# First mixers' loop: sigmoids from tanh, and the norms' inverse roots as a power on GpSimd

## What is computed

```
w  = -softplus(-(w0 + tanh(w_lo) @ w_up)) - 0.5 ; decay = exp(-exp(w))   # = exp(DECAY * sigmoid(w0 + ..))
a  = sigmoid(a0 + a_lo @ a_up)
g  = sigmoid(g_lo) @ g_up
kk = k * k_k ; kk = kk / max(sqrt(sum(kk * kk)), 1e-12)          # per head of 64
k  = k * (1 + (a - 1) * k_a) ; b_vec = kk * a
y  = recurrence over positions of (r, k, v, decay, -kk, b_vec)
y  = (head_norm(y) + bonus) * g                                  # head_norm: yc * rsqrt(mean(yc^2) + eps) * gain
ret = silu(gate_in) * head_norm(retention(q, k, v))
```

## Time and profile before

| | us |
|---|---|
| three runs | 2713.27, 2714.29, 2707.25; median 2713.27 |
| the profiled execution's own time | 2706.05 |
| its span | 2704.3 |
| busy over the span: TensorE matmul, VectorE, ScalarE, GpSimd | 2523.2, 1959.6, 1408.6, 595.2 |
| same in 500 to 600 us, two mixer turns and a part of a third | 89.75, 84.75, 80.24, 67.07 |

### The profile page before, as it was taken

One profiled execution on the slowest core, in us unless ns is written; L12 is line 12 of the kernel. 1 busy time (PEld: TensorE's weight loads), 2 busy tenths in 40 slices (PEclk: granted clock), 3 DMA queues, 4 the chain that ended last, 5 costly groups with the idle time before them and its releaser, 6 DMA issues. The chain is left out here.

```text
span 2704.3 us, 39668 instructions
## 1 busy us (share of the span) xinstructions
PE 2523.2 (93%) x14812; PEld 2065.1 (76%) x14813; DVE 1959.6 (72%) x2659; ACT 1408.6 (52%) x2172; POOL 595.2 (22%) x554
## 2 busy tenths in 40 slices
PE   8999978989897899999996899889999999999998
PEld 7988846666676688888885888668887788888776
DVE  5533147888845799999996834778778988888586
ACT  5111157787612687887785432357744433344444
POOL 0000035666601100000001500320001333432231
PEclk9999989999997899999998999999999999999999
DMA  5555321211263799999996321000221232325866
GB/s 187 192 202 219 123 90 36 74 44 63 84 236 137 278 419 412 412 412 418 414 416 228 133 60 45 1 33 32 57 94 55 78 93 62 93 86 173 208 132 183
DMA packets 168279, 454.06 MB, mean 168 GB/s; under 512 B 15260, under 2 KB 95568, under 8 KB 154832
## 3 DMA queue, kind: packets, MB, share of 16 engines
q1 hardware_dynamic: 146048, 384.62, 38.7%
q0 software_dynamic: 16336, 46.67, 6.3%
q10 hardware_dynamic: 5760, 20.97, 1.9%
HBM read 373.05 MB, written 79.17 MB: 167 GB/s over the span
## 5 line engine op out<-in xcount | busy, mean ns | idle before, releaser
L135 PE MATMUL psum<-part,expert_x_high 128*128 128x512 f32 x520 | 206.5, 397 | 2.9 <-issue 1.5
L137 PE MATMUL psum<-part,expert_x_low 128*128 128x512 f32 x520 | 203.5, 391 | 0.0
L135 PE MATMUL psum<-project_w_high,high 128*128 128x448 f32 (+1 forms) x512 | 194.6, 380 | 3.5 <-DVE low L399 3.5
L136 PE MATMUL psum<-project_w_low,high 128*128 128x448 f32 (+1 forms) x512 | 193.7, 378 | 0.0
L137 PE MATMUL psum<-project_w_high,low 128*128 128x448 f32 (+1 forms) x512 | 193.6, 378 | 0.0
L130 DVE TENSOR_TENSOR expert_down_low<-expert_down,expert_down_high 128x2048 fp32r<-128x2048 f32 x62 | 139.3, 2289 | 36.0 <-ACT expert_down_high L125 36.0
L130 DVE TENSOR_TENSOR expert_gate_low<-expert_gate,part 128x2048 fp32r<-128x2048 f32 x64 | 143.9, 2289 | 6.9 <-ACT part L125 6.2
L130 DVE TENSOR_TENSOR expert_up_low<-expert_up,part 128x2048 fp32r<-128x2048 f32 x64 | 143.8, 2289 | 1.0 <-ACT part L125 1.0
L135 PE MATMUL psum<-part,ffn_w_high 128*128 128x512 f32 x352 | 138.5, 394 | 4.1 <-DVE ffn_u L4694 3.8
L136 PE MATMUL psum<-ffn_b_low,ffn_w_high 128*128 128x512 f32 x352 | 137.9, 392 | 0.0
L135 PE MATMUL psum<-down_right_high,down_left_high 128*128 128x512 f32 x308 | 121.8, 395 | 9.5 <-DVE down_right_low L130 6.0
(11 more groups left out here) (772 smaller groups left out, 7457.5 us busy)
## 6 DMA issues: line engine op xcount, KB each, us to landing
expert_gate<-in_w_gate_dram SPq DMA_DIRECT2D x32, 2048.0 KB
expert_up<-in_w_up_dram SPq DMA_DIRECT2D x32, 2048.0 KB, 9.8
expert_down<-in_w_down_dram SPq DMA_DIRECT2D x32, 2048.0 KB, 10.7
ffn_w<-in_ffn_w_up_dram SPq DMA_DIRECT2D x44, 512.0 KB, 4.6
y_rows<-expert_y ACTq DMA_DIRECT2D x32, 512.0 KB, 10.8
down_right_raw<-in_ffn_w_down_dram SPq DMA_DIRECT2D x44, 256.0 KB, 3.7
hidden_rows<-ffn_hidden SPq DMA_DIRECT2D x20, 512.0 KB, 2.8
ffn_hidden<-hidden_rows SPq DMA_DIRECT2D x20, 512.0 KB, 6.9
```

The source lines that it names most:

```text
L135: pe.matmul(out, left[0], right[0], start=start, stop=False)
L136: pe.matmul(out, left[0], right[1], start=False, stop=False)
L137: return pe.matmul(out, left[1], right[0], start=False, stop=stop)
```

## The change

Every sigmoid of the loop becomes `0.5 * (1 + tanh(x/2))`: ScalarE takes Tanh with scale 0.5, and the missing `+1` and `0.5` are put elsewhere. For `g`, `take_lo` is now two copies, the second adding 1, and `take_g` halves. For `a`, `k_a` is halved once, `rated_b` adds the 1 in a fused operation and `tildes_ba` halves. For the decay, the 1 becomes a bias of the exponentials, from a new constant `decay_bias`. For the gate, a second ScalarE pass adds 1 in place, and `ret_gain` is halved once. The three `warm_up` calls of a turn are gone.

The three square roots of a turn leave ScalarE, and the maximum, mean-plus-eps and reciprocal steps leave VectorE. GpSimd does in their place, for each, an add or maximum and a `tensor_tensor` with `ALU.pow` against a tile of -0.5, 8 or 4 columns wide. `root_kk(t+1)` stands on GpSimd between `scale_m` and `weigh`; `rw_deviation(t-1)` and `ret_deviation(t-1)` between `open_gate` and `rw_leave`. VectorE's divide is one fused product with the square root of the width. ScalarE's y_fm copy, which overwrites the squares, and square_ret get explicit waits for the sums. The last tile's norms stay as they were.

```diff
@@ VectorE
             def unit_kk(j, u, link):
-                v.wait_ge(kk_root, 2 * j + u + 1)
-                link(v.tensor_scalar(kk_stats[:, 1, :], kk_stats[:, 1, :], 1e-12, None, ALU.max))
-                link(v.reciprocal(kk_stats[:, 2, :], kk_stats[:, 1, :]))
+                v.wait_ge(kk_root, 2 * (2 * j + u) + 2)
...
-                link(v.tensor_tensor(b_[:], kk[:], ag[:], ALU.mult))
+                link(v.scalar_tensor_tensor(out=b_[:], in0=ag[:], scalar=1.0, in1=kk[:], op0=ALU.add, op1=ALU.mult))
...
-            def spread(link, of, stats, heads, width, eps, spread_ready):
-                link(v.tensor_reduce(stats[:, 2, 0:heads], three(of, heads), AX_X, ALU.add))
-                v.tensor_scalar(stats[:, 3, 0:heads], stats[:, 2, 0:heads], 1.0 / width, eps, ALU.mult, ALU.add)\
-                    .then_inc(spread_ready, 1)
+            def spread(of, stats, heads, spread_ready):
+                v.tensor_reduce(stats[:, 2, 0:heads], three(of, heads), AX_X, ALU.add).then_inc(spread_ready, 1)
+
+            def divide(stats, heads, width, out, normed):
+                v.scalar_tensor_tensor(out=three(out, heads), in0=three(out, heads), scalar=float(np.sqrt(width)),
+                                       in1=per_row(stats[:, 5, 0:heads], width), op0=ALU.mult, op1=ALU.mult).then_inc(normed, 1)
...
             def rw_divide(t, link):
-                v.wait_ge(rw_root, t + 1)
-                norm_divide(v, link, rw_stats, RW_HEADS, RW_N, y[:], rw_normed)
+                v.wait_ge(rw_root, 2 * t + 2)
+                divide(rw_stats, RW_HEADS, RW_N, y[:], rw_normed)
...
             v.wait_ge(const, 16 * len(cn.loads))
+            v.tensor_scalar(k_a[:], k_a[:], 0.5, None, ALU.mult).then_inc(halved, 1)
@@ GpSimd
+            def root(stats, heads, add, op, t, ready):
+                of = stats[:, 2, 0:heads]
+                pool.tensor_scalar(of, of, add, None, op).then_inc(ready, 1)
+                pool.wait_ge(ready, 2 * t + 1)
+                pool.tensor_tensor(stats[:, 5, 0:heads], of, half_down[:, 0:heads], ALU.pow).then_inc(ready, 1)
...
                 scale_m(t, u)
+                if not last:
+                    root_kk(t + 1)
                 weigh(t, u)
...
                 open_gate(t, u)
                 if not first:
+                    rw_deviation(t - 1)
+                    ret_deviation(t - 1)
                     rw_leave(t - 1, 1 - u)
@@ ScalarE
             def take_lo(j, u):
                 act.wait_ge(lo_turned, 2 * j + u + 1)
-                act.activation(lo_t[:], bank[7][:, 0:256], ACT.Copy).then_inc(lo_t_ready, 1)
+                act.activation(lo_t[:, 0:P], bank[7][:, 0:P], ACT.Copy)
+                act.activation(lo_t[:, P:2 * P], bank[7][:, P:2 * P], ACT.Identity, bias=1.0).then_inc(lo_t_ready, 1)
...
-                act.activation(sg[:], p_t[:], ACT.Sigmoid).then_inc(sg_ready, 1)
+                act.activation(sg[:], p_t[:], ACT.Tanh, scale=0.5).then_inc(sg_ready, 1)
...
-                act.activation(p_t[:], bank[6][:], ACT.Exp, scale=DECAY).then_inc(exp_ready, 1)
+                act.activation(p_t[:], bank[6][:], ACT.Exp, scale=DECAY / 2, bias=decay_bias[:, 0:1]).then_inc(exp_ready, 1)
...
-                if not last:
-                    warm_up(ACT.Exp)
-                else:
+                if last:
                     early_high_of(3)
...
                     reach_ends(t + 1, 1 - u)
-                    root_kk(t + 1)
...
-                warm_up(ACT.Sigmoid)
                 act.wait_ge(q_turned, t + 1)
                 act.activation(q1[:], bank[7][:], ACT.Copy).then_inc(q1_ready, 1)
...
-                act.activation(gate[u][:], ret_in[u][:, 3 * RET_W:4 * RET_W], ACT.Sigmoid).then_inc(gate_opened, 1)
+                act.activation(gate[u][:], ret_in[u][:, 3 * RET_W:4 * RET_W], ACT.Tanh, scale=0.5).then_inc(gate_turned, 1)
                 act.wait_ge(u_made, t + 1)
                 act.activation(u_[:], bank[1][:], ACT.Copy).then_inc(u_ready, 1)
+                act.wait_ge(gate_turned, t + 1)
+                act.activation(gate[u][:], gate[u][:], ACT.Identity, bias=1.0).then_inc(gate_opened, 1)
...
-                if not first:
-                    rw_deviation(t - 1)
...
-                if not first:
-                    ret_deviation(t - 1)
                 act.wait_ge(y_made, t + 1)
+                if not first:
+                    act.wait_ge(rw_spread, t)
                 act.activation(y_fm[:], two_banks(2)[:, :, 1, :], ACT.Copy).then_inc(y_fm_ready, 1)
```

More of the change, by code:

```diff
@@ L480, in __init__ @@
         ]
-        sb("start", [P, 40])
+        sb("start", [P, 32])
         self.loaded = nc.alloc_semaphore(name="mix_consts_loaded")
@@ L905, in mean_square, with divide_last @@
                     steps[0] += 1
-                def divide(raw, stats, heads, width, n):
+                def divide_last(raw, stats, heads, width, n):
                     v.wait_ge(last_root, n)
@@ L1034, in _ @@
             sigmoid_arg_a(0, 0)
+            v.wait_ge(halved, 1)
             link = rated(0, 0)
@@ L1075, in square_kk, with root_kk, rw_deviation, ret_deviation @@
                 pool.tensor_tensor(b_[:], k_scaled[:], k_scaled[:], ALU.mult).then_inc(kk_multiplied, 1)
+            def root(stats, heads, add, op, t, ready):
[3 more added lines that the diff above has]
+                pool.tensor_tensor(stats[:, 5, 0:heads], of, half_down[:, 0:heads], ALU.pow).then_inc(ready, 1)
+            def root_kk(t):
+                pool.wait_ge(kk_squared, t + 1)
+                root(kk_stats, RW_HEADS, 1e-24, ALU.max, t, kk_root)
+            def rw_deviation(t):
+                pool.wait_ge(rw_spread, t + 1)
+                root(rw_stats, RW_HEADS, RW_N * RW_GN_EPS, ALU.add, t, rw_root)
+            def ret_deviation(t):
+                pool.wait_ge(ret_spread, t + 1)
+                root(ret_stats, RET_HEADS, RET_D * RET_GN_EPS, ALU.add, t, ret_root)
             def weigh(t, u):
@@ L1189, in squash @@
                 act.activation(lo[:, LORA:2 * LORA], f[:, 1536 + LORA:1536 + 2 * LORA], ACT.Copy).then_inc(lo_ready, 1)
[L1190 to L1194, removed]
+                act.activation(lo[:, 2 * LORA:256], f[:, 1536 + 2 * LORA:RW_COLS], ACT.Tanh, scale=0.5).then_inc(lo_ready, 1)
             def take_lo(j, u):
                 act.wait_ge(lo_turned, 2 * j + u + 1)
-                act.activation(lo_t[:], bank[7][:, 0:256], ACT.Copy).then_inc(lo_t_ready, 1)
+                act.activation(lo_t[:, 0:P], bank[7][:, 0:P], ACT.Copy)
+                act.activation(lo_t[:, P:2 * P], bank[7][:, P:2 * P], ACT.Identity, bias=1.0).then_inc(lo_t_ready, 1)
             def sigmoid_w(j, u):
@@ L1207, in sigmoid_a @@
                 act.wait_ge(a_added, t + 1)
-                act.activation(ag[:], p_inv[:], ACT.Sigmoid).then_inc(a_ready, 1)
+                act.activation(ag[:], p_inv[:], ACT.Tanh, scale=0.5).then_inc(a_ready, 1)
             def take_g(j, u, first):
@@ L1486, in _ @@
             take_lo(0, 0)
-            root_kk(0)
             sigmoid_w(0, 0)
```

65 lines of the change are left out of this document (34 added, 31 removed).

## The result

The changed kernel takes 2738.03 us (median of 4, 2735.75 to 2745.12), the kernel before, run beside it, 2713.78: a ratio of 1.0103, 95% interval 1.0085 to 1.0121. It is slower by some 1%, where no change was forecast, and outside the range of 2706 to 2726. The profiled execution took 2736.3 us with a span of 2734.1, against 2706.05 and 2704.3.

A forecast was written before the change was run, and what follows sets the result against it. It took VectorE's waits for GpSimd and TensorE's road to set the turn, most ScalarE loads being hidden. Turns 2 to 6 + 1.0, - 0.7, - 0.1, - 0.4, - 0.3 and preamble + 0.5 gave 0.0 us: 2713.3 us, range 2706 to 2726.

The forecast's parts named there:

- the term that decides: Work added on GpSimd: root_kk in front of weigh makes weigh, fade_state and rotate start 1.1 us later a turn.
- P: Price of one GpSimd power, 8 or 4 columns wide: taken as 0.5 us, between 0.20 and 1.27.
- GpSimd as the bound: Rival, slower: with P over 0.9 late roots delay rw_leave, each of five turns costs 3P - 2.1 us; chance 0.22.
- the 0.78 us: TensorE's road through a turn gets 0.78 us shorter: 0.22 from the load before q1, 0.56 from that before y_fm.
- loads (5) and (1): ScalarE table loads: before y_fm, worth 0.56 us a turn; before the packing at the turn's head, worth nothing.
- (3) and (4): ScalarE table loads: under TensorE's transposes and the state's raising, taken as 0; before q1, worth 0.22 us a turn.
- (2): ScalarE table load ahead of its share of copies: worth 0 to 0.4 us, taken as 0 because VectorE's road decides.
- State-sum wait 1.5 to 2 us: Sign: VectorE's wait at the state's sum goes up from 0.4 to about 1.5 to 2 us a turn.
- Turns of 44.1: Sign: turns of the loop take 44.1 us from t = 2, against 43.87 before.
- Preamble and turn 0 together: Preamble + 0.5 us, for halving k_a at the head of VectorE's road; turn 0, without a norm behind it, - 0.1.
- Turn 1: Turn where VectorE doesn't wait for GpSimd: - 0.7 us.
- Last turn and end of the stage together: Last turn - 0.4 us, without kk's root; end of the stage - 0.3, estimated between - 1.0 and + 1.0.

The follow-up runs named there:

- e1_product: Changed kernel with all three GpSimd powers replaced by products of the same shape; 2715.74 us, ratio 1.0030 to the kernel before.
- e10_before_power: Kernel before plus one unread 128x8 power on GpSimd between the state's scaling and the bonus product; 2722.02 us, ratio 1.0055.
- e7_probe: e1_product plus a row of powers and products of 1 to 64 columns on GpSimd ahead of the loop; one run, 2734.02 us.
- e3_kk_product: Changed kernel with only kk's power replaced by a product; one run, 2719.04 us.
- e8_gate_early: Changed kernel with root_kk moved behind fade_state, and the gate's two ScalarE passes and GpSimd product moved forward; 2713.98 us, ratio 1.0021 to the kernel before.
- e11: e8_gate_early with four TensorE stops filled by repeating work just done; 2719.5 us, ratio 1.0035 to the kernel before.
- e12: e8_gate_early with two TensorE repeats, lift 0 and the product into banks 2 and 3; 2715.35 us, ratio 1.0024 to the kernel before.
- e9: Changed kernel with TensorE's product ahead of its longest stop done three times instead of once; 2736.57 us, ratio 1.0105 to the kernel before.

## Why the prediction was wrong

**The step that failed** is the one it called the term that decides: "I take P = 0.5, nearer the row of the same shape". P measured 1.67 us at 8 columns and 1.33 at 4. Both ends given for it, 0.20 and 1.27, lay under it; the upper one was a 128x512 product, and the runs show that a power of 8 columns costs more than a product of 512. The row of the same shape was the wrong neighbour, since from 1 to 64 columns the power's time grows from 0.58 to 10.54 us where the product's stays at 0.19 to 0.32. The prediction's other figure, 0.4 us for each of a root's two operations, doubled the add as well, though the rule it quotes is for two inputs and the add has one; the add took 0.25 us, the power four times 0.4.

**The rival was right in mechanism.** GpSimd as the bound, decided from P = 1.3, had 0.22. Put the measured prices into its own sum: 1.67 - 0.3 + (1.67 + 1.33) - 1.8 = 2.6 us a turn. Measured at full clock, after is 46.93 - 44.00 = 2.9. Both of its halves are seen: the wait at the state's sum (3.10 in place of 0.40) and `rw_leave` later by 1.9 us. That the two numbers lie so close is in part luck: the sum has 2.7 for the powers and - 0.1 for the rest, the runs 2.2 and + 0.7.

**The price alone doesn't give the time.** With the measured prices, and turn 1 taken as the rival took it, the prediction's sum gives some 13 us, 2726, the upper edge of the range. Of the 29.8 us of the profiled execution 16.7 are left: 6.5 in turns 2 to 6, where the clock had part, 2.5 in turn 1, 1.5 in the preamble and turn 0, 3.2 behind the seventh copy, and 3.0 where nothing was changed.

**The signs, one by one.** Loads 40 to one or two: right. The waits of L1818 and L1691: TensorE's matmuls no longer wait there (weight loads for L1691's successor still do, 0.5 us a turn), but the 0.78 us counted for them can't be confirmed: with loads (5) and (1) back turns of equal clock were as long, with (3) and (4) back turns at 0.93 were no longer, and only turn 1 at full clock was, by 0.4. Loads (1) to (3) at zero: (1) and (3) in agreement; (2) was not tried by itself. State-sum wait 1.5 to 2 us: 3.1 with the power, 1.6 with a product (e1_product), so the road around the power was priced to some 0.4 us. Turns of 44.1: 47.6; with P at a product's 0.2 the same sum says 43.8, and at full clock they took 44.65 to 44.69. "Over 45.5, the power is dear": the sign held. Preamble and turn 0 together, forecast + 0.4: + 1.9, VectorE waiting 2.25 us for the first root, and 0.77 in e1_product, where the copy comes 0.4 later as forecast. (e10_before_power, with before's preamble, has it 1.7 earlier, so that a single execution doesn't weigh much here.) Turn 1, forecast - 0.7: + 3.0, by the powers and the clock, since with free powers at full clock it took 42.59 (e7_probe) against 42.97. There VectorE did not wait for GpSimd before, and there the power of e10_before_power cost only 43.25 - 42.97 = 0.3; from turn 2 on, where it waited 0.4 us, it cost the whole 1.7. That reading of the earlier trace rows held. Last turn and end of the stage together, forecast - 0.7: from the seventh copy to the router + 2.5, and - 1.1 with free powers (73.9 us in e1_product, 75.0 before), so that free powers make this stretch 3.6 us shorter.

**What was not in the sum at all.** First TensorE's clock. No term and no rival had it, as the profiled execution of before kept 2.4 GHz in all six turns. Second the gate: the prediction let `gate_opened` be 1.3 us late and found that free for GpSimd. It is not free for VectorE, where tilde_k beside the gate product takes 1.76 us instead of 0.68; with the gate early, 0.68 again.

**The account of a turn**, by turns at equal clock: 44.00 before; + 0.7 for the change with free powers (44.69); + 2.2 for the powers (46.93), of which 0.7 are the norms' (e3_kk_product) and so 1.5 kk's, beside 1.68 for kk's in the kernel before; + 0.8 for the clock (47.76). What makes up the 0.7 was not separated. With free powers the state's sum still waits 1.6 us in place of 0.4, for the small operation and the gaps of kk's root, which at the price seen in e10_before_power is more than the 0.7; the gate, moved in e8_gate_early, has a part as well; and what the change takes away stands against them.

**Still open.** What makes the clock fall. Filling the stops kept the clock in e11 and e12 in nearly all turns; in e9 the fall came elsewhere, longer; and the same loop had five such turns of six in e1_product and two in e7_probe. A stop of TensorE stands ahead of most falls, but not the longest one: in e7_probe both began 0.3 us after a stop of 0.83 us, while the four stops of 1.2 us in its other turns had none behind them. That any one stop causes a fall isn't shown.

## What to carry to other kernels

An operation that no row of the trace shows isn't bounded by its shape. When the whole forecast hangs on such a price, the case beyond it isn't a rival at 0.22 but half of the question, and the range must reach it. Before work goes to an engine that others wait for, look for a place with slack: one move by two lines, behind the operation that others wait for, hid the whole of kk's power. And a wait of 0.4 us for such an engine in every turn meant here that what was put in front of it was paid in full: 1.64 us of power, 1.68 us of turn.

## Not expected of the hardware

- GpSimd's power costs 0.58 us at 1 column, 1.87 at 8 (1.67 in the loop), 10.54 at 64, about 0.16 us a column; its product 0.19 to 0.32 over the same widths.
- TensorE's granted clock fell to 1.2 GHz for 3.4 to 6.8 us in all six turns after, and in three of six where the only thing added was a power on GpSimd. Such a fall can cost more than the stops of TensorE around it: a turn of the loop that e1_product and e7_probe share took 44.65 at full clock and 47.2 with a fall, and its longest stop is 1.2 us.
- A VectorE product of 128x512 took 1.76 us beside a GpSimd product of the same size, 0.68 without it. What reads as an engine's own price can be its neighbour's.
